# Attention values with V stationary in two 64-column halves of TensorE, softmax sums by GpSimd and one-row products, outputs transposed back

## The reference

```python
s_sel = jnp.where(m_sel, s_sel, NEG).reshape(b, G, HPG, QB, n_sel * SLC_LEN)
p_sel = jax.nn.softmax(s_sel, axis=-1)
o_sel = jnp.einsum('bghqnl,bgqnle->bghqe', p_sel, v_sel)
...
p_win = jax.nn.softmax(jnp.where(m_win, s_win, NEG), axis=-1)
o_win = jnp.einsum('bghqk,bgke->bghqe', p_win, v_win)
...
o = g[0] * o_cmp + g[1] * o_sel + g[2] * o_win
```

## Time and profile before

| | |
|---|---|
| median of the runs | 702.08 us (2 runs, 701.69 to 702.46) |
| the profiled execution | 701.53 us, its span 699.7 us |
| the attention stage in it | 183.8 to 282.6 us, 98.8 us |
| granted TensorE clock | 0.993 over the span, 1.00 in the stage |

### The profile page before, as it was taken

One profiled execution on the slowest core, in us unless ns is written; L12 is line 12 of the kernel. 1 busy time (PEld: TensorE's weight loads), 2 busy tenths in 40 slices (PEclk: granted clock), 3 DMA queues, 4 the chain that ended last, 5 costly groups with the idle time before them and its releaser, 6 DMA issues.

```text
span 699.7 us, 8985 instructions
## 1 busy us (share of the span) xinstructions
PE 670.9 (96%) x3571; PEld 560.4 (80%) x3571; DVE 334.2 (48%) x574; ACT 227.9 (33%) x384; POOL 187.8 (27%) x95
## 2 busy tenths in 40 slices
PE   2899999999999989999999999999999999999996
PEld 2689889887787778888988888888888888888885
DVE  4898888754587784436312522101000039633126
ACT  4546432340333424235432222222222123232224
POOL 2000000000000000050154544544444429455521
PEclk9899999999999999999999999999999999999999
DMA  9979968520000000770055445433433213232003
GB/s 310 361 272 350 386 208 275 210 90 31 0 2 1 1 1 1 254 227 1 1 150 152 136 140 162 134 91 90 112 107 104 99 60 121 91 106 75 0 1 120
DMA packets 74537, 88.08 MB, mean 126 GB/s; under 512 B 3112, under 2 KB 57600, under 8 KB 74368
## 3 DMA queue, kind: packets, MB, share of 16 engines
q1 hardware_dynamic: 73184, 85.31, 37.7%
q10 hardware_dynamic: 896, 1.12, 0.4%
q0 software_dynamic: 416, 1.08, 0.4%
HBM read 85.41 MB, written 2.10 MB: 125 GB/s over the span
## 4 chain that ended last, share of the span: by engine, by line
PE 92%; DVE 4%; issue 1%; DMA 1%; ACT 1%; SPq 0%; POOL 0%; POOLq 0%; DVEq 0%; ACTq 0%
PE ps L1232 14%; PE ps L1234 13%; PE ps L1233 13%; PE ps L1630 11%; PE ps L1632 11%; PE ps L1631 11%; PE ps L1368 5%; PE ps L1425 1%; PE ps L1317 1%; PE ps L1503 1%; DVE ps L916 1%; DMA xs<-in_x 1%; PE ps L1411 1%; PE ps L1245 1%; DVE acc L767 1%
## 5 line engine op out<-in xcount | busy, mean ns | idle before, releaser
L428 POOL TENSOR_TENSOR wl<-raw,wh 128x1024 fp32r<-128x1024 f32 x66 | 172.3, 2615 | 212.3 <-ACT wh L477 212.2
L1630 PE MATMUL ps<-hTh,wh 128*128 128x512 f32 (+1 forms) x384 | 143.6, 374 | 0.0
L1632 PE MATMUL ps<-hTh,wl 128*128 128x512 f32 (+1 forms) x384 | 142.6, 371 | 0.0
L1631 PE MATMUL ps<-hTl,wh 128*128 128x512 f32 (+1 forms) x384 | 142.6, 371 | 0.0
L477 ACT ACTIVATE wh<-raw 128x1024 fp32r<-128x1024 f32 x94 | 97.0, 1038 | 136.0 <-PE ps L1632 74.0
L1162 DVE TENSOR_TENSOR act<-ps,sg 128x512 f32<-128x512 f32 x22 | 15.2, 692 | 195.1 <-PE ps L1632 195.1
L1232 PE MATMUL ps<-wh,hTh 128*128 128x512 f32 (+2 forms) x232 | 89.9, 388 | 1.4 <-DVE hTl L821 1.4
L1233 PE MATMUL ps<-wl,hTh 128*128 128x512 f32 (+2 forms) x232 | 86.9, 374 | 0.0
L1234 PE MATMUL ps<-wh,hTl 128*128 128x512 f32 (+2 forms) x232 | 86.8, 374 | 0.0
L1631 PEld LDWEIGHTS ps<-hTl,wh 128*128 128x128 f32 x384 | 72.3, 188 | 12.9 <-issue 0.5
L1630 PEld LDWEIGHTS ps<-hTh,wh 128*128 128x128 f32 x384 | 72.3, 188 | 12.8 <-issue 0.5
(11 more groups left out here) (194 smaller groups left out, 835.3 us busy)
## 6 DMA issues: line engine op xcount, KB each, us to landing
raw<-in_w_ada SPq DMA_DIRECT2D x32, 512.0 KB, 5.3
raw<-in_w_ff_gate SPq DMA_DIRECT2D x22, 512.0 KB, 4.0
raw<-in_w_ff_up SPq DMA_DIRECT2D x22, 512.0 KB, 3.8
raw<-in_w_ff_down SPq DMA_DIRECT2D x22, 512.0 KB, 3.2
raw<-in_w_in SPq DMA_DIRECT2D x20, 512.0 KB, 7.4
early<-in_w_ada SPq DMA_DIRECT2D x16, 512.0 KB, 10.0
raw<-in_w_out SPq DMA_DIRECT2D x8, 512.0 KB, 3.8
xs<-in_x SPq DMA_DIRECT2D x4, 512.0 KB, 5.3
```

Source lines behind the costliest of these rows:

```text
L428: pool.tensor_tensor(lo, raw[:, slot, 0:n], hi.bitcast(F32), ALU.subtract).then_inc(w_lo2, 1)
L1630: mm(o, hi[:, ks], hTh[:, k, c0:c1], start=k == 0, stop=False)
L1631: mm(o, hi[:, ks], hTl[:, k, c0:c1], start=False, stop=False)
L1632: ins = mm(o, lo[:, ks], hTh[:, k, c0:c1], start=False, stop=k == KT - 1)
```

## The change

In `values`, V becomes the stationary operand (64 columns) and the weights of a step stream, 512 columns for a head group. Group g = 0 writes output partitions 0 to 63 and g = 1 partitions 64 to 127 of one bank, 2 for b = 0 and 3 for b = 1. The output is now transposed: head width on the partitions, heads and queries on the columns. The column of ones is gone. The sums are made in another way: where a group has two steps or more, POOL adds the weights of its steps, one 128 x 1024 addition for each step but the first (`weight_sum`, 12 in all); then PE multiplies the sum with a column of ones, four one-row products of 512 columns for a query tile, which go to partitions 0, 32, 64 and 96 of bank 3 (`den_sums`). ACT copies the four rows out (`den_copy`), PE transposes them (4 transposes), and DVE takes the reciprocals and multiplies by both branches' gates at once (`den_gates`). ACT copies each group's output out of PSUM (`out_copy`, 8 in all), PE transposes it (`out_transposes`, 4 each, into bank 3), and DVE multiplies it as before. Weights of steps 0 and 1 get memory of their own. The slots of most tables are set anew, and behind the stage there are six `out_unit`s (`FILL` = 3) with the work of the last query tile between them.

The diff, cut (waits that only follow from it, and declarations, are left out):

```diff
-PAIR_AT = {2: [(4, 0)], 4: [(4, 1)], 6: [(4, 2)], 7: [(4, 3)], 11: [(5, 0)], 12: [(5, 1)], 13: [(5, 2)], 14: [(5, 3)], 16: [(6, 0)], 17: [(6, 1)], 19: [(6, 2)], 21: [(6, 3)], 24: [(7, 0)], 26: [(7, 1)], 29: [(7, 2), (7, 3)]}
-MAX_AT = {0: 2, 2: 3, 9: 4, 15: 5, 22: 6, 30: 7}
-CS_AT = {9: 2, 21: 3}
-CT_AT = {13: 2, 23: 3}
-CO_AT = {0: 1, 16: 2, 25: 3}
-RS_AT = {8: (1, 0), 10: (1, 1), 18: (2, 0), 20: (2, 1), 27: (3, 0), 28: (3, 1)}
-RV_AT = {2: [(0, 0), (0, 1)], 10: [(1, 0)], 13: [(1, 1)], 19: [(2, 0)], 21: [(2, 1)], 29: [(3, 0)], 30: [(3, 1)]}
-SQ_AT = {3: 0, 13: 1, 21: 2, 30: 3}
-NORM_AT = {5: 0, 15: 1, 23: 2, 38: 3}
-M_AT = {7: 0, 17: 1, 27: 2}
-OUT_AT = {17: 0, 20: 1, 27: 2, 34: 3}
+PAIR_AT = {1: [(4, 0)], 4: [(4, 1)], 5: [(4, 2)], 8: [(4, 3)], 11: [(5, 0)], 13: [(5, 1)], 14: [(5, 2), (5, 3)], 16: [(6, 0)], 17: [(6, 1)], 19: [(6, 2)], 21: [(6, 3)], 24: [(7, 0)], 26: [(7, 1)], 29: [(7, 2), (7, 3)]}
+MAX_AT = {0: 2, 2: 3, 9: 4, 15: 5, 23: 6, 31: 7}
+CS_AT = {14: 2, 23: 3}
+CT_AT = {19: 2, 28: 3}
+CO_AT = {0: 1, 20: 2, 29: 3}
+RS_AT = {10: (1, 0), 12: (1, 1), 20: (2, 0), 21: (2, 1), 27: (3, 0), 28: (3, 1)}
+RV_AT = {0: [(0, 0), (0, 1)], 15: [(1, 0)], 16: [(1, 1)], 23: [(2, 0)], 24: [(2, 1)], 33: [(3, 0)], 34: [(3, 1)]}
+SQ_AT = {2: 0, 16: 1, 25: 2, 35: 3}
+NORM_AT = {4: 0, 16: 1, 26: 2, 40: 3}
+M_AT = {10: 0, 21: 1, 31: 2}
+OUT_AT = {18: 0, 20: 1, 26: 2, 33: 3}
+ENDS = STEP0[2::2]
+DEN_AT = {6: 0, 14: 1, 26: 2}
+DENT_AT = {7: 0, 16: 1, 27: 2}
+OT_AT = {8: 0, 9: 1, 17: 2, 18: 3, 28: 4, 29: 5}
+SUMMED = [n for x in range(2, GROUPS) for n in range(STEP0[x] + 1, STEP0[x + 1])]
+FILL = 3
...
@@ sync
                     sp.wait_ge(st_ps, NG * STEPS)
                     sp.wait_ge(cs_ps, TT)
+                    sp.wait_ge(den_ps, TT)
...
@@ gpsimd
+            def weight_sum(n):
+                x, j = step(n)
+                i, b = divmod(x, 2)
+                pool.wait_ge(p_exp, NG * (n + 1))
+                if j == 1:
+                    pool.wait_ge(den_ps, i)
+                else:
+                    pool.wait_ge(p_sum, sum_count(n) - 1)
+                pool.tensor_tensor(sums(x), weights(n - 1) if j == 1 else sums(x), weights(n), ALU.add).then_inc(p_sum, 1)
...
@@ scalar
             def exp(n):
                 for g in range(NG):
                     a.wait_ge(st_ps, NG * n + g + 1)
-                    if n == 1:
+                    if n == 3:
                         a.wait_ge(r_y, 2)
-                    if n >= 2:
+                    if n >= 4:
                         a.wait_ge(pv, n - 1)
-                    a.activation(PT[:, n % 2, g, :], ps[:, g, :], ACT.Exp, scale=-1.0).then_inc(p_exp, 1)
+                        a.wait_ge(p_sum, sum_count(n - 2 if n - 2 in SUMMED else n - 1))
+                    a.activation(weights(n)[:, g], ps[:, g, :].rearrange("p (h q) -> p h q", h=HPG), ACT.Exp, scale=-1.0).then_inc(p_exp, 1)
+            def out_copy(x):
+                a.wait_ge(pv, STEP0[x + 1])
+                if x >= 2:
+                    a.wait_ge(o_T, x - 1)
+                a.activation(OT[:, x % 2, :], ps[:, 2 + x % 2, :], ACT.Copy).then_inc(oT_ok, 1)
+            def den_copy(i):
...
+                a.activation(denR[:, :], ps[:, 3, :], ACT.Copy).then_inc(den_ok, 1)
...
@@ vector
+            def den_gates(i):
...
+                ins = d.reciprocal(r, den)
...
+                then(d.tensor_tensor(rgt[:, :], rgt[:, :], gates[:, i, NH:3 * NH], ALU.mult))
             def add_branch(x):
-                i, b = divmod(x, 2)
-                d.wait_ge(pv, STEP0[x + 1])
-                then(d.reciprocal(r, o[:, :, :, DH]))
-                then(d.tensor_tensor(rgt[:, :], rgt[:, :], gates[:, i, (b + 1) * NH:(b + 2) * NH], ALU.mult))
+                d.wait_ge(o_T, x + 1)
...
@@ tensor
             def values(n):
...
-                if j == 0 and x:
-                    pe.wait_ge(o_read, x)
-                for g in range(NG):
-                    pe.wait_ge(p_exp, NG * n + g + 1)
-                    for h in range(HPG):
-                        ins = mm(ps[:, 2 + g, h * DE:(h + 1) * DE], PT[:, n % 2, g, h * P:(h + 1) * P], V[:, j, b, g, :],
-                                 start=j == 0 and h == 0, stop=j == i and h == HPG - 1)
+                if j == 0 and x >= 2:
+                    if b:
+                        pe.wait_ge(o_read, x - 1)
+                    else:
+                        pe.wait_ge(oT_ok, x - 1)
+                pe.wait_ge(p_exp, NG * (n + 1))
+                for g in range(NG):
+                    ins = mm(ps[g * DH:(g + 1) * DH, 2 + b, :].rearrange("p (h q) -> p h q", h=HPG), V[:, j, b, g, :], weights(n)[:, g],
+                             start=j == 0, stop=j == i)
                 ins.then_inc(pv, 1)
+            def den_sums(i):
+                pe.wait_ge(oT_ok, 2 * i + 2)
...
+                for b in range(2):
+                    for g in range(NG):
+                        c = CP * (NG * b + g)
+                        ins = mm(ps[c:c + 1, 3, :].rearrange("p (h q) -> p h q", h=HPG), ones[:, 0:1], sums(2 * i + b)[:, g], start=True, stop=True)
+                ins.then_inc(den_ps, 1)
+            def den_transposes(i):
+                pe.wait_ge(den_ok, i + 1)
+                for h in range(HPG):
+                    ins = pe.transpose(ps[:, 3, h * P:(h + 1) * P], denR[:, h * P:(h + 1) * P], ident)
...
+            def out_transposes(x):
+                pe.wait_ge(oT_ok, x + 1)
...
+                for h in range(HPG):
+                    ins = pe.transpose(ps[:, 3, h * P:(h + 1) * P], OT[:, x % 2, h * P:(h + 1) * P], ident)
...
-            for k in range(2):
+            out_unit(0, 0)
+            den_sums(TT - 1)
+            out_unit(2, 0)
+            den_transposes(TT - 1)
+            out_unit(0, 1)
+            out_transposes(GROUPS - 2)
+            out_unit(2, 1)
+            out_transposes(GROUPS - 1)
+            for k in range(2, FILL):
                 for t in (0, 2):
                     out_unit(t, k)
             mix_transposes(TT - 1)
             pe.wait_ge(o_read, GROUPS)
-            out_unit(1, 0)
-            out_unit(1, 1)
+            for k in range(FILL):
+                out_unit(1, k)
             pe.wait_ge(mix_lo, TT)
```

More of the change, by code:

```diff
@@ L47 @@
 SPLIT = 4
-DE = DH + 1
 GROUPS = 2 * TT
@@ L217, in block_kernel @@
         gates = small("gates", [P, TT, 3 * NH])
-        rgt = small("rgt", [P, NH])
+        rgt = small("rgt", [P, 2 * NH])
         mnc = small("mnc", [P, NH])
@@ L232, in ats, with sums, weights @@
             return hTf[:, p, :, (TT - 1) * P:T].rearrange("p (a j) q -> p a j q", a=2)
+        def sums(x):
+            i, b = divmod(x, 2)
+            if i < 2:
+                return hTf[:, b, :, 2 * P:3 * P].rearrange("p (g h) q -> p g h q", g=NG)
+            return QTf[:, b].rearrange("p h (t q) -> p t h q", q=P)[:, 0:NG]
+        def weights(n):
+            return sums(n) if n < 2 else PT[:, n % 2].rearrange("p g (h q) -> p g h q", h=HPG)
         rope = cst[:, K_ROPE:K_ROPE + TT * P].rearrange("p (t n) -> p t n", t=TT)
@@ L308, in step, with sum_count @@
             return g, n - STEP0[g]
+        def sum_count(n):
+            return SUMMED.index(n) + 1
         def pair_count(g, h):
@@ L443, in _ @@
             pool.memset(mcol[:, :, :], 0.0).then_inc(mcol_set, 1)
-            for i in range(TT):
-                power(N_RET + i, yss[:, :])
+            def weight_sum(n):
+                x, j = step(n)
+                i, b = divmod(x, 2)
+                pool.wait_ge(p_exp, NG * (n + 1))
[4 more added lines that the diff above has]
+                pool.tensor_tensor(sums(x), weights(n - 1) if j == 1 else sums(x), weights(n), ALU.add).then_inc(p_sum, 1)
+            for n in range(SLOTS):
+                if n - 1 in SQ_AT:
+                    power(N_RET + SQ_AT[n - 1], yss[:, :])
+                if n % 2 == 0 and n // 2 in SUMMED:
+                    weight_sum(n // 2)
             for u in range(U0_GU, UNITS):
@@ L618, in ret_squares @@
                 a.wait_ge(r_y, 2 * (i + 1))
+                if len(squared) > 1:
+                    a.wait_ge(denT_ps, squared[-1] + 1)
+                squared[0] = i + 1
                 for h in range(RH):
@@ L653, in _ @@
             for n in range(SLOTS):
+                if n % 2 == 0 and n // 2 - 1 in STEP0[1:]:
+                    out_copy(STEP0.index(n // 2 - 1) - 1)
                 if n % 2 == 0 and n // 2 < STEPS:
                     exp(n // 2)
+                if n in DEN_AT:
+                    den_copy(DEN_AT[n])
                 if n - 1 in CS_AT:
@@ L665, in _ @@
                     high(U0_OUT + OUT_AT[n])
+            out_copy(GROUPS - 1)
+            den_copy(TT - 1)
             mix_high(TT - 1)
@@ L1076, in _ @@
             for n in range(SLOTS):
-                if n % 2 and n // 2 in STEP0[1:]:
-                    add_branch(STEP0.index(n // 2) - 1)
+                if n in OT_AT:
+                    add_branch(OT_AT[n])
```

(24 more changed lines are left out.)

40 lines of the change are left out of this document (31 added, 9 removed).

## The result

The kernel after the change takes 714.51 us (median of two runs, 714.29 to 714.74) beside 702.08: a ratio of 1.0173, 95% interval 1.0153 to 1.0194. It is slower, and 3.5 us beyond the upper end of the range. Its profiled execution has a span of 712.2 us, 12.5 more than before. The change does what it says: V is stationary in two halves, and the step of the values takes half its time. The time was lost elsewhere.

A forecast was written before the change was run, and what follows sets the result against it. PE was taken to bound the kernel, values holding 37.7% of the stage's chain. PE -7.7, ACT +0.5, POOL +2.5, behind the stage +0.3: -4.4 from 701.53, forecast 697 us; own range 692 to 701, 8-in-10 range 688.5 to 711.

The forecast's parts named there:

- Values: Values on PE: column halves run side by side, a step takes 0.96 us against 1.93, twenty steps -19.4 us.
- Both rivals with less overlap: Values and sums on PE: halves do not overlap, 721.5 us, chance 0.12; half-overlap by order, 709, chance 0.08.
- Sums, transposes, turns: Work added to PE's list: one-row products for the sums +4.2 us, 48 transposes +5.3, turns between forms +2.2.
- Behind the stage: After the attention stage: the last tile's work lies between six output units and costs +0.3 us.
- The ten waits I leave at 14 us: Attention stage's chain: PE's ten waits, 1.2 to 2.2 us each, stay at some 14 us together.
- The upper bound of +4: Attention stage: the ten waits grow by +4 us at most, judged from DVE's share of busy time.
- The new slots at nothing: Attention stage: new slots move row minima and retention scores apart in places; no cost was put on them, 0.
- PE has its full clock throughout: PE, whole kernel before: clock at its upper level, 2.4 GHz, so nothing to gain by a longer clock.
- POOL's additions: Attention stage: 12 additions of 128 x 1024, about 2.6 us each, mostly hidden; exponentials waiting for them cost +2.5 us.
- step 18: Attention stage: nothing lies in this step's slots, so the exponentials' wait for POOL's addition is not hidden, 1.7 us.
- the gain is lost to the engines beside PE: Rival, attention stage: the 7.7 us go into new waits for POOL, ACT and DVE; 702 us, chance 0.18.
- the 7.7 us of net gain: PE's list in the attention stage: -19.4 values, +4.2 sums, +5.3 transposes, +2.2 turns, net -7.7 us.

The follow-up runs named there:

- the ladder: Kernels between the one before and the one after, each with one more layer of the change; neighbours' differences price the layers, which sum to +12.1 us.
- c3: Kernel after without additions, the sums' path and the outputs' copies and transposes, all slots and order as before: 0.9848 of the kernel before.
- a2: Kernel after with all 12 additions at full size, but over the sums' own memory, so no exponential waits for them: 1.0118 of the kernel before.
- e3: Kernel after with 56 zero matmuls in PE's waits, e1's 41 and 15 more in slot 21: 1.0098 of the kernel before, 709.0 us.
- e1: Kernel after with 41 zero matmuls on PE just ahead of seven places where it waits for DVE: 1.014 of the kernel before, 711.9 us.

## Why the prediction was wrong

- **Values** (right): -18.6 us (20 x 0.93) against -19.4; the halves overlap. Both rivals with less overlap are out. The lower ratio of 2.38 for three column tiles, which the prediction took from the Trainium skill, "TensorE: Matmul & The Clock Gate", Measured speedup vs the span model, is not borne out for two halves: 1.01 us a step is 0.05 over the full overlap with its turn, where that ratio gave an estimate of 1.08 for the streams alone.
- **Sums, transposes, turns** (right): +6.3 and +4.3 by the ladder, +6.3 and +4.8 forecast. ACT's copies cost nothing of their own. Behind the stage +2.7 us, against 2.8 of PE work for the last tile and 0.3.
- **"The ten waits I leave at 14 us"** (the step that failed first). These were the chain's pieces outside PE, not time in which PE stood: it stood for 98.80 - 93.03 = 5.8 us, and the rest was covered by its other work, the values of 1.94 us among it. The bare swap with everything in its old place gives 10.7 of 18.0 us. I took DVE's share of 0.73 in a shorter stage for room. In c3 DVE's share is 64.79 / 89.0 = 0.73, just that, and it holds 34 us of the chain. The share said how long DVE works, not how late its answers come: a row minimum, a scaling of an output unit and a branch stand in one list, and the values of 1.94 us had covered them. With 1.01 they no longer do. The upper bound of +4 for this term, which no row gave, was too low by half: it is +7.3, of which 0.8 is the values' own.
- **The new slots at nothing** (failed): +8.4 in the form without sums and transposes, a large part of it through the clock. I weighed two tables in words and no table's place against the time at which DVE comes to it.
- **"PE has its full clock throughout"** (failed): I read it as a state that would last. In the kernel before PE stood for 5.8 us in all and 1.5 at most at a time; in the kernel after for 15.4 and 2.5, and the clock fell three times. Filled waits gave 5.3 us back. They are part of the 12.1 and not a sum beside it; the clock first falls in the slots' row.
- **POOL's additions** (size nearly right, mechanism wrong): 3.8 against 2.5. No exponential waited for them, at step 18 or elsewhere. By the trace they held DVE up, which the prediction did not price; how the 3.8 us divide is open (a2).
- The rival "the gain is lost to the engines beside PE" was the right mechanism at the wrong price: it stopped at 702 because it let the waits eat the 7.7 us of net gain and no more. They can eat the whole gain of the shorter values, and PE's additions then stand on top: -10.7 + 10.6 + 3.8 alone is +3.7, and the slots' 8.4 come on top.

Open: how the 8.4 us of the slots divide in the whole change, where clock and waits can't be pulled apart by tables alone; and what a schedule made for this form, with DVE's list in the order in which PE needs it, would give. The lowest time found with all of the work done in the new form is e3's, 709.0 on the scale used here; the kernel before is faster than each of them.

## What to carry to other kernels

When the longest item on the bounding engine is halved, first take the chain again with that item at its new length: whatever answered within the old one and not within the new is on the path, however modest the answering engine's share of busy time. Price extra items at full (they came out so here) and expect less than the full saving until that is done (here 10.7 of 18.0 us). And an engine at full clock in the kernel before may lose it when its waits change. Their sum did not decide it here: c3 kept the full clock with 8.7 us of them in the stage, and e1 had 6.8 us at the lower level with 7.4. Where the waits can't be shortened, work that does nothing can be cheaper than standing.

## What was not expected

Adding 13 us of idle matmuls made a kernel 5.3 us faster (e3). A 16-column product took 1.65 us instead of 0.18 beside an addition on POOL, while one from PSUM kept its 0.69. Float32 matmuls of two passes in two column halves overlap as fully as row halves: four records of 512 columns in 1.01 us.
